# Gate tiles through ScalarE's queue, and DMA additions moved from the weight sums to the branch merge

## The chip, the cores and the metric

One core of a Trainium2 chip runs the whole kernel. The metric is the time of one execution on the device, in microseconds (us). The engines that matter here are TensorE (PE; PEld is its weight load), VectorE (DVE), ScalarE (ACT), GpSimd (POOL) and SyncE (SP). SP, ACT and POOL each have a queue from which they issue DMA transfers; a transfer issued from POOL's queue can add to its destination instead of overwriting it.

## What is computed

One layer of a hybrid decoder for 512 prompt tokens and 8 sample tokens (520 columns). The part that the change touches is the merge of the two token mixers:

```python
mix = jax.nn.sigmoid(g_a) * (o_a @ w_proj_gmlp) + jax.nn.sigmoid(g_b) * (o_b @ w_proj_nsa)
x = x + mix @ w_out
```

`o_a` and `o_b` have 1024 channels, `mix` has 2048. Everything is fp32. A product is made of three TensorE passes over operands that are split into a high part and a rest: high by high, high by rest, rest by high. ScalarE writes the high part of a weight tile (`hi`), VectorE subtracts it from the tile to get the rest (`lo`).

## The kernel before

Activations stay in SBUF as 16 tiles of 128 channels by 520 columns. Weights stream from HBM into the four slots of `w_raw` (512 KB each) by SP's queue.

**Pairs.** A stretch of the kernel works in 22 *pairs* (class `Pair`, number `n`). Each pair multiplies a 2 by 2 block of weights by a 2 by 2 block of operands with seven products instead of eight (the Winograd form of Strassen's scheme), so it needs four sums of weight quarters: `a11+a21`, `a22` plus that, `a21+a22`, and `a12` plus the second. They are the helper `st_sums` with step 0 to 3, on VectorE. Pairs 0 to 13 make gate columns `g_a` and `g_b`, whose sigmoids are stored to the DRAM tensor `merge_d`. Pairs 14 to 21 are the eight *parts* 0 to 7 (`p.part = n - 14`). Parts 0 to 3 are the four quarters `q` of the gMLP projection; their results lie in `mix_a[q]`. Parts 4 to 7 are the four quarters of the sparse-attention projection; their results lie in `b_f`. `N_PROJ = 8`, `N_ST = 14`, `N_PAIRS = 22`.

**The seven products of a pair** run in a fixed order on TensorE. Product `k` waits for `ff_lo` to reach `p.e + k + 1`, that is for the rest of weight entry `k`. The helper `ring_in(p, k)` exists twice: on ScalarE it writes the high part of entry `k`, on VectorE the rest. Entries 0, 1 and 6 are raw slots; 2 and 5 come from the buffer `st_sum` (the second and the fourth sum); 3 and 4 are sums in place in `w_raw`. An entry's buffer is one of three, so it is free when the product three entries earlier is done. ScalarE's `st_copy(p, 0..3)` and VectorE's `st_added(p, 0..2)` drain PSUM; product 4 waits for `st_copy(p, 1)`, product 3 for `st_added(p, 0)`.

**Two sums by DMA.** From pair `N_SUMMED = 12` on (`loaded_sums`), the third and the fourth sum are not made on VectorE: `low_sum` and `wide_sum` on POOL's queue load the same weight quarter once more from HBM and add it to `w_raw[:, 2]` and to `st_sum`. `wide_sum` may start when the rest of entry 2 is written, and entry 5 waits for its landing (semaphore `wide_summed`).

**Gates.** `load_gates(p)` on POOL's queue brings the four gate tiles of a part from `merge_d` to SBUF (1040 KB), into `g_in0`, `g_in1` or `g_late`, once the gates that lay there before are used. POOL's loop issues them in the same in-order queue, right behind `low_sum` of the next pair and ahead of `wide_sum` of the next pair. For part 4 two of them stand there one behind the other.

**Merge.** VectorE's `gate(p, t_)` multiplies two result tiles by their gates. From part 4 on, `merge(p, t_)` on VectorE then adds the two tiles of `mix_a` to those of `b_f`; ScalarE's `b_hi_in` and VectorE's `b_lo_in` split the sum into the operand of the output projection. In parts 5 to 7 these belong to the part before (`old`), and they stand in the instruction order between the weight entries: on VectorE gate 0 ahead of entry 2, merge 0 ahead of entry 3, gate 1 and merge 1 ahead of entry 5, `b_lo_in` ahead of and behind entry 6; on ScalarE `b_hi_in(old, 0)` between entry 4 and `st_copy(p, 1)`, `b_hi_in(old, 1)` between entry 6 and `st_copy(p, 3)`. Part 7 itself is gated, merged and split behind the last pair. After that the output projection (L1010) starts; its fourth chunk of weights waits for the last `b_lo_in`.

Of the kernel before, what the change touches and what calls it, by code (L numbers as in the profile page):

```python
# [57 lines left out]
N_ST = 14  # L58
# [6 lines left out]
U_PROJ = U_GATE + 2 * M_ST  # L65
N_PROJ = 8
N_PAIRS = N_ST + N_PROJ
N_SUMMED = 12
U_OUT = U_PROJ
U_FF = U_OUT + MB  # L70
UNITS = U_FF
# [62 lines left out]

def base_of(g, k):

    first = 2 * (N_PAIRS + N_SUMMED) if COUNTS[k] == "sums" else N_PAIRS * U_COUNTS[k]
    return first if whole(g, 0) else BODY_TOTAL[k] * g + (first + FIRST_TOTAL[k] - BODY_TOTAL[k])


# [4 lines left out]
class Pair:  # L145


    def __init__(self, n):
        self.n, self.part = n, n - N_ST
        self.phase, self.q = divmod(self.part, N_PROJ // 2)  # L150
        self.e, self.used, self.copied, self.c21, self.read, self.sums = (n * c for c in U_COUNTS)
        self.loaded_sums, turn = n >= N_SUMMED, n - N_SUMMED
        if self.loaded_sums:
            self.sums = 4 * N_SUMMED + 2 * turn
            self.summed = 16 * turn + 16

    def ring(self, k):

# [147 lines left out]
def build(nc, t):  # L306
    with ExitStack() as ctx:
# [455 lines left out]
        def gates_home(p):  # L763
            return g_late if p.part == N_PROJ // 2 else g_in[p.part % 2]
# [823 lines left out]
        def _(act):  # L1588
# [239 lines left out]

            def b_hi_in(p, t_):

                act.wait_ge(b_mixed, 2 * p.q + t_ + 1)
                run(mixed_part(b_hi, p, t_), mixed_part(b_f, p, t_), ACT.Copy).then_inc(b_split, 1)

            def st_scaled(j):
# [100 lines left out]
            ring_in(p, 0, (chunk_done, CH * (U_PROJ - 1) + 2))  # L1935
            ring_in(p, 1, (chunk_done, CH * U_PROJ))

            def first_free(p, k):

                return (b_ready, 2) if p.ring(k) == LATE and p.last_free(k) is None else None  # L1940

            def st_pair(p):
                old = Pair(p.n - 1) if p.n else None
                js = slice(2 * p.part - 2, 2 * p.part)
                if old:
                    st_c21(old)
                ring_in(p, 2, None if old else (chunk_done, CH * U_PROJ))
                if p.part == 0:
                    gm_hi(T3)
                st_copy(p, 0)  # L1950
                ring_in(p, 3, None if old else (chunk_done, CH * U_PROJ))
                if p.part == -1:
                    gm_hi(B11)
                if p.part == 0:
                    gm_hi(B22)
                if p.part in (1, 2):
                    nsa_hi(B11, js)
                ring_in(p, 4)
                if p.part > 4:
                    b_hi_in(old, 0)  # L1960
                if not old:
                    gate_out(2 * M_ST - 1)
                if p.part == -1:
                    gm_hi(B21)
                if p.part == 0:
                    gm_hi(T4)
                if p.part in (1, 2):
                    nsa_hi(B21, js)
                if p.part == 3:
                    nsa_hi(T2)  # L1970
                if old and p.part < 0:
                    st_tanh(old, 0)
                st_copy(p, 1)
                ring_in(p, 5)
                if old and p.part < 0:
                    st_tanh(old, 1)
                if p.part in (1, 2):
                    nsa_hi(B22, js)
                if p.part == 3:
                    nsa_hi(T3)  # L1980
                st_copy(p, 2)
                ring_in(p, 6)
                if p.part > 4:
                    b_hi_in(old, 1)
                if p.part == -1:
                    gm_hi(T2)
                if p.part == 0:
                    st_tanh(old, 0)
                if p.part in (1, 2):
                    nsa_hi(T1, js)  # L1990
                if p.part == 3:
                    nsa_hi(T4)
                st_copy(p, 3)
                if p.part < N_PROJ - 1:
                    to = Pair(p.n + 1)
                    ring_in(to, 0, first_free(to, 0))
                    if p.part == -1:
                        gm_hi(T1)
                    if p.part == 0:
                        st_tanh(old, 1)  # L2000
                    ring_in(to, 1, first_free(to, 1))
# [200 lines left out]
        def _(dve):  # L2202
# [640 lines left out]
            def merge(p, t_):  # L2843

                dve.wait_ge(gated, KP + 2 * p.part + t_ + 1)
                y = st_out(p, t_)
                dve.tensor_tensor(y, y, mix_a[p.q][:, t_:4:2, :], ALU.add).then_inc(b_mixed, 1)

            def st_pair(p):
# [3 lines left out]
                if old:  # L2853
# [24 lines left out]
                    if p.part == 4:  # L2878
                        gate(older, 1)
                    if p.part > 4:  # L2880
                        merge(old, 0)
                    ring_in(p, 3)
                if not p.loaded_sums:
                    st_sums(p, 3)
# [22 lines left out]
                    gate(older, 1)  # L2907
                if p.part == 4:
                    gate(old, 0)
                if p.part > 4:  # L2910
                    gate(old, 1)
                    merge(old, 1)
                if old and p.part < -1:
                    st_scale(old, 1)
                elif not old:
# [372 lines left out]
        def _(pool):  # L3288
# [205 lines left out]
            def wide_sum(p):  # L3494

                pool.wait_ge(ff_lo, p.e + 3)
                pool.dma_start(st_sum[:, :], t["w_st"][4 * p.n + 1], accum_op=ALU.add).then_inc(wide_summed, 16)

            def load_gates(p):
                for t_ in range(2):  # L3500
                    pool.wait_ge(g_stored[t_], 64 * (p.q + 1))
                pool.dma_start(gates_home(p)[:, :, :], merge_d.rearrange("(q k t) p n -> t q p k n", k=4, t=2)[
                    p.phase][p.q]).then_inc(g_loaded[p.part % 2], 16)

            for n in range(N_SUMMED - 2):
                for p in range(2):
# [2 lines left out]
            for n in range(N_SUMMED - 1, N_PAIRS):  # L3509
                p, old, to = Pair(n), Pair(n - 1), Pair(n + 1)  # L3510
                if p.loaded_sums:
                    wide_sum(p)
                if p.part <= 0:
                    gate_half(M_ST + n - 1, 0, st_out(old, 0))
                if p.part < 0:
                    gate_half(M_ST + n - 1, 1, st_out(old, 1))
                if p.part < N_PROJ - 1:
                    low_sum(to)
                if p.part == 0:
                    gate_half(M_ST + n - 1, 1, st_out(old, 1))  # L3520
                    pool.wait_ge(ff_used, old.used + NP)
                    load_gates(p)
                if p.part == 1:
                    pool.wait_ge(mix_lo, GM_DONE)
                    load_gates(p)
                if p.part in (2, 3):
                    pool.wait_ge(gated, KP + 2 * p.part - 2)
                    load_gates(p)
                if p.part == 3:
                    pool.wait_ge(ff_used, p.used + NP)  # L3530
                    load_gates(to)
                if p.part in (4, 5, 6):
                    pool.wait_ge(gated, KP + (8, 6, 12)[p.part - 4])
                    load_gates(to)
            pool.wait_ge(b_ready, N_PROJ)
            steps.did(pool.memset(acc_x[:, :], 0.0))

# [187 lines left out]
```

## Time and profile before

| | us |
|---|---|
| median of 3 runs | 2603.17 |
| lowest and highest | 2601.89, 2608.93 |
| the profiled execution's own time | 2605.25 |
| its span, from the first to the last instruction | 2603.8 |
| mean granted TensorE clock, share of full speed | 0.996 |

A profile is one execution. Times in its rows count from the start of the span. A line such as `1038.38 0.80 PE L1403 ... [6.27 <-DVE w_lo L2752]` says: at 1038.38 us an instruction of line 1403 began on PE and ran 0.80 us; before it PE stood idle for 6.27 us, which ended when the VectorE instruction of line 2752 that wrote `w_lo` signalled. Buffer numbers are left out in the names, and buffers that lie in the same memory can appear under the name of another (`a_hi`, `late_hi` and `w_hi` are all weight buffers in this stretch).

### The profile page before, as it was taken

How to read it: one execution, taken by the hardware profiler on the slowest of the kernel's cores; microseconds unless marked ns; L12 is line 12 of the kernel's file. 1: busy time of each engine (PE TensorE's matmuls, PEld its weight loads, DVE VectorE, ACT ScalarE, POOL GpSimd, SP SyncE). 2: the span in 40 equal slices, each digit the busy share in tenths (PEclk: the TensorE clock that was granted, in tenths of full speed). 3: DMA queues.
4: the chain of work that ended last, by engine and by line, in shares of the span. 5: the costliest groups of instructions: out<-in, count | busy, mean ns of one | idle time of the engine just before them, and what ended most of it. 6: DMA issues, size and time to landing. Idle time of an engine off the chain costs nothing. (4 is left out here: it accounts for less than half of the span.)

```text
span 2603.8 us, 56700 instructions
## 1 busy us (share of the span) xinstructions
PE 2573.6 (99%) x21295; PEld 2544.3 (98%) x21295; DVE 2019.4 (78%) x2903; ACT 1448.5 (56%) x2441; POOL 479.1 (18%) x641
## 2 busy tenths in 40 slices
PE   9999999999999998999999999999999999999998
PEld 9999999999999998999999999999999999999998
DVE  6455646668777787865688889888898888898888
ACT  6445436556444464432366666566666665666656
POOL 2001350001121221123302121121211211212113
PEclk9999999999999999999999999999999999999999
DMA  6633552213343466643336675665756657667568
GB/s 212 203 113 115 165 172 74 66 53 129 129 143 132 146 181 194 187 139 132 131 106 151 164 175 141 169 156 153 182 144 168 163 145 173 152 164 174 140 171 178
DMA packets 128089, 389.45 MB, mean 150 GB/s; under 512 B 14450, under 2 KB 16114, under 8 KB 127696
## 3 DMA queue, kind: packets, MB, share of 16 engines
q1 hardware_dynamic: 69328, 245.36, 28.0%
q0 software_dynamic: 55456, 136.73, 24.7%
q10 hardware_dynamic: 3168, 5.45, 0.6%
q8 instruction: 95, 1.56, 0.2%
q14 instruction: 42, 0.34, 0.0%
HBM read 302.77 MB, written 91.00 MB: 151 GB/s over the span
## 5 line engine op out<-in xcount | busy, mean ns | idle before, releaser
L3017 DVE TENSOR_TENSOR w_lo<-w_raw,w_hi 128x1024 fp32r<-128x1024 f32 x351 | 428.7, 1223 | 104.6 <-ACT w_hi L2031 104.0
L2031 ACT ACTIVATE w_hi<-w_raw 128x1024 fp32r<-128x1024 f32 x352 | 370.9, 1062 | 200.9 <-PE aux L1454 69.1
L1454 PE MATMUL aux<-at_t,w_hi 128*128 128x260 f32 x2016 | 368.0, 282 | 0.2 <-DVE w_lo L3017 0.2
L2208 DVE TENSOR_TENSOR w_lo<-w_raw,w_hi 128x512 fp32r<-128x512 f32 x216 | 158.8, 738 | 257.2 <-ACT w_hi L1599 256.5
L1518 PE MATMUL aux<-fb_mid,w_hi 128*128 128x260 f32 x1920 | 352.2, 284 | 1.4 <-DVE w_lo L3017 1.1
L1599 ACT ACTIVATE w_hi<-w_raw 128x512 fp32r<-128x512 f32 x216 | 135.2, 628 | 316.1 <-PE mm L1010 293.9
L1454 PEld LDWEIGHTS aux<-at_t,w_hi 128*128 128x128 f32 x2016 | 310.6, 188 | 0.4 <-DVE w_lo L3017 0.4
L1518 PEld LDWEIGHTS aux<-fb_mid,w_hi 128*128 128x128 f32 x1920 | 295.1, 188 | 2.7 <-DVE w_lo L3017 1.3
L1454 PE MATMUL aux<-at_t,w_lo 128*128 128x260 f32 x1008 | 284.5, 282 | 0.0
L1518 PE MATMUL aux<-fb_mid,w_lo 128*128 128x260 f32 x960 | 270.7, 282 | 0.0
L1518 PE MATMUL mm<-fb_mid,w_hi 128*128 128x260 f32 x1440 | 263.9, 282 | 0.0
L1010 PE MATMUL mm<-a_hi,w_hi 128*128 128x260 f32 x1216 | 254.5, 291 | 0.0
L1010 PE MATMUL mm<-a_hi,w_lo 128*128 128x260 f32 x1216 | 244.8, 283 | 0.0
L1010 PE MATMUL mm<-a_lo,w_hi 128*128 128x260 f32 x1216 | 244.4, 283 | 0.0
L1518 PEld LDWEIGHTS mm<-fb_mid,w_hi 128*128 128x128 f32 x1440 | 222.0, 188 | 0.0
L3579 POOL TENSOR_TENSOR cell<-cell 128x1 f32<-128x1 f32 x62 | 20.8, 335 | 1054.0 <-ACT y_mid L2084 1042.1
L1454 PE MATMUL mm<-at_t,w_hi 128*128 128x260 f32 x1120 | 204.8, 283 | 0.7 <-ACT hid L2067 0.7
L1518 PE MATMUL mm<-fb_mid,w_lo 128*128 128x260 f32 x720 | 203.7, 283 | 0.0
L1010 PEld LDWEIGHTS mm<-a_hi,w_hi 128*128 128x128 f32 x1216 | 187.9, 189 | 5.6 <-issue 3.8
L1454 PEld LDWEIGHTS aux<-at_t,w_lo 128*128 128x128 f32 x1008 | 189.6, 188 | 0.0
L1010 PEld LDWEIGHTS mm<-a_lo,w_hi 128*128 128x128 f32 x1216 | 187.4, 188 | 0.0
L1010 PEld LDWEIGHTS mm<-a_hi,w_lo 128*128 128x128 f32 x1216 | 187.4, 188 | 0.0
(600 smaller groups left out, 6865.8 us busy)
## 6 DMA issues: line engine op xcount, KB each, us to landing
w_raw<-in_w_ff SPq DMA_DIRECT2D x256, 512.0 KB, 3.6
out_y_t<-y_mid POOLq DMA_DIRECT2D x120, 520.0 KB, 8.0
w_raw<-in_w SPq DMA_DIRECT2D x110, 512.0 KB, 3.7
w_raw<-in_w_st SPq DMA_DIRECT2D x88, 512.0 KB, 5.0
g_in<-merge_d POOLq DMA_DIRECT2D x7, 1040.0 KB, 10.0
w_raw<-in_w_st POOLq DMA_DIRECT2D x10, 512.0 KB, 5.4
st_sum<-in_w_st POOLq DMA_DIRECT2D x10, 512.0 KB, 8.5
merge_d<-z POOLq DMA_DIRECT2D x18, 260.0 KB, 4.0
```

The source lines that it names most:

```text
L1010: last = pe.matmul(mm[:, 2 * v + h, 0:HT], w, a[:, kt, h * HT:(h + 1) * HT], start=first and k == 0 and part == 0, stop=final and k == CK ...
L1454: last = pe.matmul(dst, w, at_of(j)[:, e:e + HT], start=FRESH[b] and j == 0 and part == 0, stop=j == KP - 1 and part == 2, skip_group_chec ...
L1518: last = pe.matmul(dst, w, fb[:, j, e:e + HT], start=FRESH[b] and j == 0 and part == 0, stop=j == 1 and part == 2, skip_group_check=not FR ...
L1599: run(w_hi[:, c, :], raw(u, c), ACT.Copy).then_inc(hi_split, 1)
L2031: run(hi_of(p, k), source(p, k), ACT.Copy).then_inc(ff_hi, 1)
L2208: dve.tensor_tensor(w_lo[:, c, :], raw(u, c), w_hi[:, c, :].bitcast(F32), ALU.subtract).then_inc(lo_split, 1)
L3017: dve.tensor_tensor(lo_of(p, k), source(p, k), hi_of(p, k).bitcast(F32), ALU.subtract).then_inc(ff_lo, 1)
L3579: pool.tensor_tensor(cell[:, 2:3], cell[:, 0:1], cell[:, 1:2], ALU.mult).then_inc(cell_step, 1)
```

## The change

Three things are changed together.

1. `load_gates` moves from POOL's queue to ScalarE's. ScalarE issues the gates of each part from inside that part, behind the high part of entry 5 (behind entry 6 in part 3).
2. In parts 5, 6 and 7 (`n >= N_MERGED = 19`) no sum is added by DMA: VectorE makes all four (`st_sums` 2 and 3 as in pairs 0 to 11).
3. In parts 5 to 7 the merge of the part before leaves VectorE: `merged` on POOL's queue adds the two tiles of `mix_a` to those of `b_f` by a DMA from SBUF to SBUF, and `b_hi_in` waits for its landing. Gate 1 moves up to the place where merge 0 stood. Part 7 is still merged on VectorE.

```diff
--- before.py
+++ after.py
@@ -65,7 +65,7 @@
 U_PROJ = U_GATE + 2 * M_ST
 N_PROJ = 8
 N_PAIRS = N_ST + N_PROJ
-N_SUMMED = 12
+N_SUMMED, N_MERGED = 12, N_ST + 5
 U_OUT = U_PROJ
 U_FF = U_OUT + MB
 UNITS = U_FF
@@ -134,7 +134,7 @@
 
 def base_of(g, k):
 
-    first = 2 * (N_PAIRS + N_SUMMED) if COUNTS[k] == "sums" else N_PAIRS * U_COUNTS[k]
+    first = Pair(N_PAIRS).sums if COUNTS[k] == "sums" else N_PAIRS * U_COUNTS[k]
     return first if whole(g, 0) else BODY_TOTAL[k] * g + (first + FIRST_TOTAL[k] - BODY_TOTAL[k])
 
 
@@ -149,10 +149,9 @@
         self.n, self.part = n, n - N_ST
         self.phase, self.q = divmod(self.part, N_PROJ // 2)
         self.e, self.used, self.copied, self.c21, self.read, self.sums = (n * c for c in U_COUNTS)
-        self.loaded_sums, turn = n >= N_SUMMED, n - N_SUMMED
-        if self.loaded_sums:
-            self.sums = 4 * N_SUMMED + 2 * turn
-            self.summed = 16 * turn + 16
+        self.loaded_sums, turn = N_SUMMED <= n < N_MERGED, n - N_SUMMED
+        self.sums = 4 * n - 2 * min(max(turn, 0), N_MERGED - N_SUMMED)
+        self.summed = 16 * turn + 16
 
     def ring(self, k):
 
@@ -1828,7 +1827,10 @@
 
             def b_hi_in(p, t_):
 
-                act.wait_ge(b_mixed, 2 * p.q + t_ + 1)
+                if p.part == N_PROJ - 1:
+                    act.wait_ge(b_mixed, t_ + 1)
+                else:
+                    act.wait_ge((low_summed, wide_summed)[t_], Pair(p.n + 1).summed)
                 run(mixed_part(b_hi, p, t_), mixed_part(b_f, p, t_), ACT.Copy).then_inc(b_split, 1)
 
             def st_scaled(j):
@@ -1935,6 +1937,23 @@
             ring_in(p, 0, (chunk_done, CH * (U_PROJ - 1) + 2))
             ring_in(p, 1, (chunk_done, CH * U_PROJ))
 
+            GATES_USED = {2: 2, 3: 4, 5: 8, 6: 6, 7: 12}
+
+            def load_gates(p):
+
+                for t_ in range(2):
+                    act.wait_ge(g_stored[t_], 64 * (p.q + 1))
+                if p.part == 0:
+                    act.wait_ge(ff_used, Pair(N_ST - 1).used + NP)
+                elif p.part == 1:
+                    act.wait_ge(mix_lo, GM_DONE)
+                elif p.part == 4:
+                    act.wait_ge(ff_used, Pair(p.n - 1).used + NP)
+                else:
+                    act.wait_ge(gated, KP + GATES_USED[p.part])
+                act.dma_start(gates_home(p)[:, :, :], merge_d.rearrange("(q k t) p n -> t q p k n", k=4, t=2)[
+                    p.phase][p.q]).then_inc(g_loaded[p.part % 2], 16)
+
             def first_free(p, k):
 
                 return (b_ready, 2) if p.ring(k) == LATE and p.last_free(k) is None else None
@@ -1972,6 +1991,8 @@
                     st_tanh(old, 0)
                 st_copy(p, 1)
                 ring_in(p, 5)
+                if p.part >= 0 and p.part != 3:
+                    load_gates(p)
                 if old and p.part < 0:
                     st_tanh(old, 1)
                 if p.part in (1, 2):
@@ -1980,6 +2001,8 @@
                     nsa_hi(T3)
                 st_copy(p, 2)
                 ring_in(p, 6)
+                if p.part == 3:
+                    load_gates(p)
                 if p.part > 4:
                     b_hi_in(old, 1)
                 if p.part == -1:
@@ -2878,7 +2901,7 @@
                     if p.part == 4:
                         gate(older, 1)
                     if p.part > 4:
-                        merge(old, 0)
+                        gate(old, 1)
                     ring_in(p, 3)
                 if not p.loaded_sums:
                     st_sums(p, 3)
@@ -2907,9 +2930,6 @@
                     gate(older, 1)
                 if p.part == 4:
                     gate(old, 0)
-                if p.part > 4:
-                    gate(old, 1)
-                    merge(old, 1)
                 if old and p.part < -1:
                     st_scale(old, 1)
                 elif not old:
@@ -3496,11 +3516,11 @@
                 pool.wait_ge(ff_lo, p.e + 3)
                 pool.dma_start(st_sum[:, :], t["w_st"][4 * p.n + 1], accum_op=ALU.add).then_inc(wide_summed, 16)
 
-            def load_gates(p):
-                for t_ in range(2):
-                    pool.wait_ge(g_stored[t_], 64 * (p.q + 1))
-                pool.dma_start(gates_home(p)[:, :, :], merge_d.rearrange("(q k t) p n -> t q p k n", k=4, t=2)[
-                    p.phase][p.q]).then_inc(g_loaded[p.part % 2], 16)
+            def merged(p, t_):
+
+                pool.wait_ge(gated, KP + 2 * p.part + t_ + 1)
+                y = st_out(p, t_)
+                pool.dma_start(y, mix_a[p.q][:, t_:4:2, :], accum_op=ALU.add).then_inc((low_summed, wide_summed)[t_], 16)
 
             for n in range(N_SUMMED - 2):
                 for p in range(2):
@@ -3510,28 +3530,17 @@
                 p, old, to = Pair(n), Pair(n - 1), Pair(n + 1)
                 if p.loaded_sums:
                     wide_sum(p)
+                if p.part > 4:
+                    for t_ in range(2):
+                        merged(old, t_)
                 if p.part <= 0:
                     gate_half(M_ST + n - 1, 0, st_out(old, 0))
                 if p.part < 0:
                     gate_half(M_ST + n - 1, 1, st_out(old, 1))
-                if p.part < N_PROJ - 1:
+                if n + 1 < N_MERGED:
                     low_sum(to)
                 if p.part == 0:
                     gate_half(M_ST + n - 1, 1, st_out(old, 1))
-                    pool.wait_ge(ff_used, old.used + NP)
-                    load_gates(p)
-                if p.part == 1:
-                    pool.wait_ge(mix_lo, GM_DONE)
-                    load_gates(p)
-                if p.part in (2, 3):
-                    pool.wait_ge(gated, KP + 2 * p.part - 2)
-                    load_gates(p)
-                if p.part == 3:
-                    pool.wait_ge(ff_used, p.used + NP)
-                    load_gates(to)
-                if p.part in (4, 5, 6):
-                    pool.wait_ge(gated, KP + (8, 6, 12)[p.part - 4])
-                    load_gates(to)
             pool.wait_ge(b_ready, N_PROJ)
             steps.did(pool.memset(acc_x[:, :], 0.0))
```

## Rows read from the trace of the kernel before

**Rows 1.** The page, busy time of each engine.

```profile
PE 2573.6 (99%) x21295; PEld 2544.3 (98%) x21295; DVE 2019.4 (78%) x2903; ACT 1448.5 (56%) x2441; POOL 479.1 (18%) x641
```

**Rows 2.** Stretches: pair 13; 15 to 17; 18; 19; 20; 21. Length, busy by engine, PEclk, DMA.

```profile
908.50:928.60 20.10, 20.10 (x170) 20.10 (x169) 18.61 (x20) 14.03 (x18) 7.11 (x8) 1.00 0.69 184
948.70:1017.20 68.50, 63.08 (x510) 62.48 (x509) 53.95 (x54) 36.71 (x48) 9.18 (x12) 0.98 0.67 193
1017.20:1046.70 29.50, 22.93 (x168) 22.45 (x166) 19.54 (x20) 9.68 (x12) 4.97 (x6) 0.88 0.63 185
1046.70:1067.00 20.30, 20.30 (x172) 20.30 (x171) 17.44 (x17) 11.73 (x14) 0.84 (x1) 1.00 0.66 201
1067.00:1094.40 27.40, 23.14 (x169) 22.85 (x169) 21.54 (x22) 11.68 (x14) 4.10 (x5) 0.88 0.57 156
1094.40:1118.20 23.80, 21.88 (x170) 21.67 (x169) 18.27 (x19) 11.99 (x16) 0.87 (x1) 0.93 0.66 187
```

**Rows 3.** Timeline of PE, pair 18 and the start of the output projection.

```profile
1038.38 0.80 PE L1403 MATMUL mm<-nsa_t,w_hi 128*128 128x260 f32 x2 [6.27 <-DVE w_lo L2752]
1038.98 0.42 PE L1403 MATMUL mm<-nsa_t,w_lo 128*128 128x260 f32 x1
...
1118.26 0.40 PE L1010 MATMUL mm<-b_hi,w_hi 128*128 128x260 f32 x2
```

**Rows 4.** Timeline of POOL: DMA issues in pairs 13 and 18.

```profile
912.29 0.88 POOL L3497 DMA_DIRECT2D st_sum<-in_w_st  x1 [4.18 <-DVE a_lo L2752]
...
1018.74 0.79 POOL L3502 DMA_DIRECT2D g_in<-merge_d  x1 [0.20 <-issue]
1019.51 0.80 POOL L3502 DMA_DIRECT2D g_late<-merge_d  x1
1022.94 0.91 POOL L3497 DMA_DIRECT2D st_sum<-in_w_st  x1 [2.62 <-DVE w_lo L2752]
```

**Rows 5.** Timeline of ACT: entry 5 of pairs 13 and 18.

```profile
917.73 1.07 ACT L1907 ACTIVATE a_hi<-st_sum 128x1024 fp32r<-128x1024 f32 x1
...
1036.01 1.06 ACT L1907 ACTIVATE w_hi<-st_sum 128x1024 fp32r<-128x1024 f32 x1 [9.56 <-DMA st_sum<-in_w_st]
```

**Rows 6.** The page's DMA issues: queue, count, size, median us to landing.

```profile
out_y_t<-y_mid POOLq DMA_DIRECT2D x120, 520.0 KB, 8.0
...
g_in<-merge_d POOLq DMA_DIRECT2D x7, 1040.0 KB, 10.0
w_raw<-in_w_st POOLq DMA_DIRECT2D x10, 512.0 KB, 5.4
st_sum<-in_w_st POOLq DMA_DIRECT2D x10, 512.0 KB, 8.5
```

**Rows 7.** Line 912, SP's 84 weight loads among the pairs: time to landing.

```profile
DMA to landing us min/median/max: 3.0/5.0/10.3
```

**Rows 8.** Timeline of DVE, pair 20 and the end of pair 21.

```profile
1068.70 1.22 DVE L2765 TENSOR_TENSOR st_sum<-w_raw 128x1024 f32<-128x1024 f32 x1
1069.83 1.24 DVE L2841 TENSOR_TENSOR b_f<-b_f,g_in 128x1040 f32<-128x1040 f32 x1
1071.05 1.22 DVE L2752 TENSOR_TENSOR w_lo<-st_sum,w_hi 128x1024 fp32r<-128x1024 f32 x1
1072.19 1.24 DVE L2847 TENSOR_TENSOR b_f<-b_f,mix_a 128x1040 f32<-128x1040 f32 x1
...
1074.76 0.69 DVE L2780 TENSOR_TENSOR b_f<-b_f,mm 128x520 f32<-128x520 f32 x1
...
1116.79 1.24 DVE L2841 TENSOR_TENSOR b_f<-b_f,g_in 128x1040 f32<-128x1040 f32 x1
...
1122.86 2.47 DVE L2663 TENSOR_TENSOR b_lo<-b_f,b_hi 128x1040 fp32r<-128x1040 f32 x2
```

**Rows 9.** Timeline of ACT, pair 20.

```profile
1074.44 1.06 ACT L1832 ACTIVATE b_hi<-b_f 128x1040 fp32r<-128x1040 f32 x1
1075.73 0.60 ACT L1921 ACTIVATE b_f<-mm 128x520 f32<-128x520 f32 x1 [0.23 <-PE mm L1403]
1083.46 1.06 ACT L1907 ACTIVATE w_hi<-st_sum 128x1024 fp32r<-128x1024 f32 x1 [7.12 <-DMA st_sum<-in_w_st]
```

**Rows 10.** Line 1656, issues on ACT's own queue: duration of one, ns.

```profile
L1656 ACTq DMA_DIRECT2D out_kv_t<-z x10: 338/338/339, 56.2 to 161.2; - x10
```

## The prediction

> **What bounds the kernel now.** First the page: TensorE is busy for 99% of the span [rows 1], so a change can win only where TensorE idles or runs slowly. Next the stretches of the pairs. Pair 13 has its sums from DMA and no gates in the way: 20.1 us, all of it busy, clock 1.00 [rows 2]. That is 2.87 us a product. Against 20.1 us a pair, pairs 15 to 17 lose 68.5 - 60.3 = 8.2, pair 18 9.4, pair 19 0.2, pair 20 7.3, pair 21 3.7: 28.8 us, nearly all that this stage can give back. Part of it is clock: in pair 18 TensorE is idle for 29.5 - 22.93 = 6.6 of the 9.4 lost, and the matmuls that follow the idle time take 0.42 us with a mean granted clock of 0.88 [rows 2, 3].
>
> Then who ends the idle time. TensorE waits for the rest of entry 5 [rows 3], VectorE for its high part, and ScalarE for the landing of `wide_sum` (9.56 us in pair 18, 7.12 in pair 20) [rows 5, 9]. Last the queue: in pair 13 `wide_sum` is issued at 912.29 and ScalarE goes on at 917.73 without a wait, at most 5.4 us later. In pair 18 two gate loads go out at 1018.74 and 1019.51; `wide_sum` follows at 1022.94 and ScalarE goes on at 1036.01, 13.1 us later [rows 4, 5]. Five of the seven pairs that lose time show this chain; the reader is to see 5.4 us without gates and a median of 8.5 with them [rows 6].
>
> **The change part by part.** T is the start of a pair's first product.
>
> *Gates leave POOL's queue (parts 0 to 4).* Nothing then stands between `low_sum` and `wide_sum`. In pair 18 `wide_sum` is issued at T + 5.7; landed in 5.4 it is there at T + 11.1. High part 1.06 and rest 1.22 make T + 13.4; product 5 is due at 5 x 2.87 = 14.4. One us to spare, where 13.1 us brought the rest to about T + 21. So the loss goes in pairs 15 to 18: 8.2 + 9.4 = 17.6 us. Bounds: 0 if `wide_sum` lands as late as now, 17.6 if it lands in 5.4 to 6.4. I take 17.6, since pair 13 is the same pair without gates. Late next would be the rest of product 6, whose entry is a raw slot and early.
>
> *The issue on ScalarE.* An issue on its queue takes 0.34 us [rows 10], eight of them 2.7 us. Each stands behind the high part of entry 5 and ahead of `st_copy(p, 2)`, which can't run before T + 11.5 and is due at T + 14.4: hidden by products 4 and 5. Without that cover it costs 0.34 a pair. Its own waits (stores of gates, earlier gates used) name work that is done by then: part 2's gate 1 stands ahead of entry 5 on VectorE, which product 5 needs anyway. Behind it wait `st_copy(p, 2)`, entry 6 and `b_hi_in`.
>
> *The gates' traffic.* The 1040 KB now start at about T + 11 to 13 and meet the loads of the next pair's slots. The latest of these, the fourth slot, is issued behind entry 6 at about T + 15.5 and is read by the next pair's second sum. That sum 1.22, high part 1.06 and rest 1.22 must be done at the next T + 5.7, so the slot may land at the next T + 2.2, which is 6.8 us after its issue. Loads in this stretch land in 3.0 to 10.3, median 5.0 [rows 7]. Bounds: 0 to 3.5 us a pair; I take 0, since the median is below 6.8.
> By the Trainium skill ("DMA: Bandwidth & Descriptors", "Issuing engines are not separate DMA queues") transfers from any engine share the same 16 DMA engines, and another issuer saves only issue time. By that the 1040 KB cost the same wherever they are issued; here they also move in time, behind `wide_sum`, which the rule does not price. It is the second rival below.
>
> *Parts 5 to 7, VectorE.* Two sums (1.13 us from start to start) come, two merges (1.14 to 1.15) go: equal work [rows 8]. A pair then has on VectorE seven rests at 1.14, four sums at 1.13, three additions at 0.69, two gates and two `b_lo_in` at 1.15: 19.2 us of 20.1.
>
> *Parts 5 to 7, the new wait.* `wide_sum` is gone here, and with it 0.2 + 7.3 + 3.7 = 11.2 us. In its place ScalarE waits at `b_hi_in(old, 0)` for a DMA that starts behind gate 0. Queued behind it on ScalarE are `st_copy(p, 1)`, which product 4 needs, entry 5, and the gates. Call L the time from gate 0's end to the merge's landing. The rest of entry 5 can start L + 1.06 + 0.60 + 1.06 = L + 2.7 after gate 0 [rows 9]. Meanwhile VectorE has rest 2, gate 1, rest 3, sum 4, an addition and rest 4: 1.14 + 1.15 + 1.14 + 1.13 + 0.69 + 1.14 = 6.4. So it idles L - 3.7, and its round takes 19.2 + L - 3.7 = 15.5 + L. Above L = 4.6 that is longer than TensorE's 20.1, and VectorE sets the pace.
> The first of the three pairs has a start ahead: VectorE can begin behind the previous sixth product (T - 2.9), and after high part and rest 1, two sums and gate 0 it is at T - 2.9 + 1.06 + 1.22 + 1.13 + 1.13 + 1.24 = T + 2.9; product 4 is due at T + 11.5, and `st_copy(p, 1)` is ready at T + 2.9 + L + 1.66. It loses nothing up to L = 6.9.
> No DMA of before goes from SBUF to SBUF with an addition. Nearest rows: additions into SBUF of 512 KB, 5.4 alone, 13.1 at worst [rows 4 to 6]; additions of 520 KB from SBUF to DRAM, median 8.0 [rows 6]. At L = 5.4 the round is 20.9, at 8.0 23.5, at 13.1 28.6. I take 5.8: destination and size are those of the 5.4, with a little for the second merge right behind. Round 21.3: 1.2 us lost in pairs 20 and 21 each, 2.4, and 0.2 for clock. Saved in the three pairs: 11.2 - 2.6 = 8.6. With L = 5.4 it is 9.6; with 8.0, 1.2 + 3.4 + 3.4 and about 1 us of clock for each stall (pairs 15 to 17: 5.4 idle, 8.2 lost, three stalls), 11: nothing saved.
>
> *End of the stage.* Part 7's gates now start inside pair 21 at about T + 12.3 and land some 8 to 10 us later (10.0 was the median behind POOL [rows 6]), T + 20.3 to 22.3. Before, gate 0 ran at 1116.79, 1.5 us ahead of the first output product at 1118.26; the last `b_lo_in` ended at 1125.33, and the fourth chunk was due at 1118.26 + 3 x 2.87 = 1126.9, 1.6 us later [rows 3, 8]. At T + 20.3 the gates are 1.7 us later than gate 0 was: 0.1 lost. At T + 22.3, 2.1. I take 0.5.
>
> **Sum.** 17.6 + 8.6 - 0.5 = 25.7 us. The profiled execution took 2605.25, so 2579.6; it lies 2.1 above the median of the runs shown, on which the sum gives 2603.2 - 25.7 = 2577.5, said as 2578.
>
> **The rivals.**
> - *The merge by DMA is slow (L of 8 and more).* For it: 8.0 is the median of the same bytes out of SBUF, and two merges follow each other. Against it: 5.4 into SBUF. The last three pairs then lose about what they lose now: 2603.2 - 17.6 + 0.5 = 2586.
> - *The gates only move their delay.* For it: loads that share with gates take up to 10.3 us [rows 7]. Against it: pair 18 moves 185 GB/s at a DMA share of 0.63 [rows 2], so there is room; pair 13's 184 hold with no loss. If the fourth slot lands in 8 us, the next pair loses 1.2, in seven pairs some 8: 2586. The skill's rule speaks for this rival.
> - *Slower: the same slot lands at 10.3 in every pair.* Then 3.5 and about 1 us of clock for seven pairs make 31: 2609. It decides from 6.8 us on and ends above before from some 9.5 us on. Against it: 10.3 is the maximum of 84, a median of 5.0.
> - *The change does not do what it says: `wide_sum` is late because of SP's loads, not because of gates.* Then pairs 15 to 18 stay as they are and only the last three win: 2603.2 - 8.1 = 2595. Against it: pairs 13 and 14 have the same SP loads and no wait.
>
> **How the numbers follow.** Chances: forecast 0.64, slow merge 0.14, moved delay 0.13, no effect of the gates 0.05, slower 0.04. The forecast's own range is 2574 (all 28.8 gone) to 2584. The range 2572 to 2595 takes in the run spread of before below and the first, second and fourth cases above; it leaves out the slower one and tails of the others, about 0.15. What a measurement can tell from no change is 0.3%, 8 us. Faster: forecast and the first two rivals, less their tails, and half of the fourth, 0.90; same 0.06; slower 0.04.
>
> **What the profile would show.** Right: stretches of pairs 15 to 18 of 20.1 to 20.6 us at clock 1.00; ScalarE without a wait for `st_sum`; `wide_sum` landing in 5 to 6.5 us; gates on ACT's queue, landing by the next T + 1; three merges of two each on POOL with landings near 5.8; a ScalarE wait of a few us for them ahead of `b_hi`, VectorE idle by 2 us ahead of entry 5, pairs 20 and 21 at about 21.3. Wrong: VectorE's second sum waiting for a `w_raw` load (moved delay); `b_hi` waiting 4 us and more (slow merge); the first output products idling for `b_lo` (late gates of part 7).

## The result, and the profile after

The changed kernel takes 2586.12 us (median, 2585.00 to 2587.42), the kernel before 2603.01 beside it: a ratio of 0.9931 [0.9914, 0.9948]. It is faster by 16.9 us, where 25.7 were forecast (2578). The stated range of 2572 to 2595 holds the measured time; the forecast's own range of 2574 to 2584 does not. The profiled execution took 2585.23 us (2579.6 forecast for it) with a span of 2583.8, 20.0 less than that of before; 8.2 of them are TensorE's busy time, the rest idle time gone; compare [rows 1]:

```profile
PE 2565.4 (99%) x21295; PEld 2535.6 (98%) x21295; DVE 2019.6 (78%) x2903; ACT 1451.5 (56%) x2441; POOL 470.0 (18%) x633
```

The same stretches as in [rows 2], cut at the first product of each pair: pairs 15 to 17, 18, 19, 20, 21.

```profile
948.88:1009.45 60.57, 60.57 (x507) 60.44 (x505) 55.83 (x56) 37.41 (x47) 7.88 (x10) 1.00 0.77 214
1009.45:1029.60 20.15, 20.15 (x171) 20.15 (x169) 17.21 (x17) 10.26 (x12) 0.87 (x1) 1.00 0.76 211
1029.60:1050.79 21.19, 20.52 (x170) 20.14 (x168) 16.64 (x16) 12.25 (x15) 2.41 (x2) 1.00 0.69 200
1050.79:1074.69 23.90, 21.15 (x169) 20.44 (x169) 19.28 (x18) 11.38 (x14) 2.36 (x2) 1.00 0.62 178
1074.69:1098.03 23.34, 20.95 (x171) 20.44 (x169) 19.96 (x20) 11.89 (x16) 2.36 (x2) 1.00 0.63 183
```

Pairs 15 to 18 run without a gap, as forecast: 0.2 us lost there instead of 17.6. The last three lose 1.1 + 3.8 + 3.2 = 8.1 us, where 2.6 were forecast and 11.1 were lost before. So in the two profiled executions the gates of parts 0 to 4 brought 17.3 of their 17.6 us and the last three pairs 3.0 instead of 8.6.

The page's DMA issues of the changed kernel answer to [rows 6]: `wide_sum` lands in 5.5 us instead of 8.5.

```profile
g_in<-merge_d ACTq DMA_DIRECT2D x7, 1040.0 KB, 7.4
...
st_sum<-in_w_st POOLq DMA_DIRECT2D x7, 512.0 KB, 5.5
b_f<-mix_a POOLq DMA_DIRECT2D x6, 520.0 KB, 7.0
```

Where TensorE stands still in pair 20 (timeline of PE): at the third product, for the rest of entry 2, and at the fourth, for `st_added(p, 0)`. Neither was forecast as a place of loss.

```profile
1058.42 0.51 PE L1402 MATMUL mm<-nsa_t,w_hi 128*128 128x260 f32 x2 [1.43 <-DVE w_lo L2775]
...
1062.54 0.48 PE L1402 MATMUL mm<-nsa_t,w_hi 128*128 128x260 f32 x2 [1.00 <-DVE b_f L2803]
```

VectorE's idle time in the same pair (timeline of DVE): 1.60 us behind the chain of the first merge, as forecast (1.6 for a merge that lands 5.3 us behind gate 0's end), but also 2.47 for the second merge's `b_hi` and 0.43 for the next pair's slot 0. ScalarE's rows show what it waited for.

```profile
1065.13 1.22 DVE L2775 TENSOR_TENSOR w_lo<-st_sum,w_hi 128x1024 fp32r<-128x1024 f32 x1 [1.60 <-ACT w_hi L1909]
...
1071.12 1.24 DVE L2686 TENSOR_TENSOR b_lo<-b_f,b_hi 128x1040 fp32r<-128x1040 f32 x1 [2.47 <-ACT b_hi L1834]
...
1073.40 1.23 DVE L2775 TENSOR_TENSOR late_lo<-w_raw,late_hi 128x1024 fp32r<-128x1024 f32 x1 [0.43 <-ACT late_hi L1909]
```
```profile
1048.42 1.06 ACT L1909 ACTIVATE w_hi<-w_raw 128x1024 fp32r<-128x1024 f32 x1 [1.99 <-DMA w_raw<-in_w_st]
...
1062.59 1.08 ACT L1834 ACTIVATE b_hi<-b_f 128x1040 fp32r<-128x1040 f32 x1 [4.17 <-DMA b_f<-mix_a]
...
1070.01 1.08 ACT L1834 ACTIVATE b_hi<-b_f 128x1040 fp32r<-128x1040 f32 x1 [2.77 <-DMA b_f<-mix_a]
...
1072.31 1.06 ACT L1909 ACTIVATE late_hi<-w_raw 128x1024 fp32r<-128x1024 f32 x1 [0.73 <-DMA w_raw<-in_w_st]
```

These waits look like the whole cause. The experiments show that the merges' two are not all of it.

### The profile page after: what moved, and what is told of

Read it like the earlier page. It is cut to its first block and busy times, and to the rows that moved or that the text cites. A ratio compares the mean times of both kernels' runs of the same rounds, so it can differ in the third digit from the quotient of the medians.

```text
span 2583.8 us, 56703 instructions
## 1 busy us (share of the span) xinstructions
PE 2565.4 (99%) x21295; PEld 2535.6 (98%) x21295; DVE 2019.6 (78%) x2903; ACT 1451.5 (56%) x2441; POOL 470.0 (18%) x633
```

## The experiments

"Lost" is what the pairs take above 20.12 us each, from the starts of their first products, in the one profiled execution of each run; that of e6 is 3.4 us above the run's median and that of e5 1.8. The kernel before loses 17.6 and 11.1.

| run | median us | ratio to before | lost, pairs 15 to 18 | pairs 19 to 21 |
|---|---|---|---|---|
| changed kernel | 2586.12 | 0.9931 [0.9914, 0.9948] | 0.2 | 8.1 |
| e1 gates only | 2577.44 | 0.9891 [0.9876, 0.9906] | 0.6 | 0.0 |
| e2 merge swap only | 2607.13 | 1.0001 [0.9992, 1.001] | 19.9 | 12.8 |
| e3 gates on POOL, behind `wide_sum` | 2584.48 | 0.9917 [0.9903, 0.993] | 4.6 | 2.8 |
| e4 gates on ScalarE, early | 2599.55 | 0.9978 [0.9967, 0.9988] | 15.0 | 7.8 |
| e5 changed, late parts' gates early | 2582.55 | 0.9914 [0.9901, 0.9928] | 0.1 | 5.9 |
| e6 changed, merges on VectorE | 2583.53 | 0.9918 [0.9904, 0.9931] | 0.9 | 7.8 |
| e7 sums and merges by DMA | 2587.97 | 0.9935 [0.9922, 0.9949] | 0.8 | 9.8 |
| e8 changed kernel again | 2584.67 | 0.9922 [0.9908, 0.9935] | 0.3 | 8.0 |
| e9 no merge | 2584.46 | 0.9915 [0.9898, 0.9931] | 0.4 | 7.0 |
| e10 first merge only | 2583.09 | 0.9911 [0.9895, 0.9928] | 0.3 | 5.7 |
| e11 second merge only | 2586.39 | 0.9922 [0.9906, 0.9939] | 0.5 | 8.5 |
| e12 no merge, no late gates | 2579.39 | 0.9903 [0.9886, 0.9919] | 0.3 | 1.6 |

### The two halves apart: e1 and e2

e1 is the kernel before with the gates on ScalarE's queue, sums and merges untouched:

```diff
 # ScalarE, in each part (entry 6 in part 3)
                 ring_in(p, 5)
+                if p.part >= 0 and p.part != 3:
+                    load_gates(p)
 # POOL: every wait and load_gates removed
```

> The kernel before with the gate loads moved to ScalarE's queue, and nothing else: two sums by DMA in all parts, merges on VectorE. In the changed kernel the parts' eight pairs take 169.3 us, 8.3 above eight clean ones; 8.1 of these lie in the last three pairs. Theory A (the merge by DMA is what still costs: with wide_sum landing in 5.4 us the last three pairs would be as clean as 15 to 18): eight pairs 161 to 163 us, time some 6 to 8 us below the changed kernel, about 2579. Theory B (the last three pairs needed the swap, because the gates' bytes or VectorE's 19.2 us a pair hold them up anyway): last three pairs lose 8 us or more, time 2586 or above.

e2 is the changed kernel with the gates put back on POOL's queue, at their old places.

> The changed kernel with the gate loads back on POOL's queue where they stood (behind low_sum of the next pair, in the last parts behind the two merges): only the swap of sums and merges is left. Both theories: pairs 15 to 18 lose their 17 to 18 us again. If the swap by itself wins what the prediction gave it (8.6 us in the last three pairs), the time is about 2594; if it wins only the 3.3 us that the last three pairs gained in the changed kernel, about 2600; if the gates behind the merges delay the next part, 2603 or more.

e1 takes 2577.44 us, 0.9891 [0.9876, 0.9906], near the 2579 of its theory A (the cause that this names is taken up below), and apart from 0.5 us in pair 15 all seven pairs run at TensorE's pace. Windows of pairs 15 to 17, 18, 19, 20, 21 of e1:

```profile
948.97:1009.86 60.89, 60.84 (x506) 60.51 (x505) 56.14 (x57) 37.32 (x47) 7.87 (x10) 1.00 0.78 213
1009.86:1030.01 20.15, 20.15 (x171) 20.15 (x170) 17.21 (x17) 10.23 (x12) 1.73 (x2) 1.00 0.74 211
1030.01:1050.12 20.11, 20.11 (x170) 20.11 (x169) 19.45 (x19) 12.04 (x14) 1.72 (x2) 1.00 0.73 210
1050.12:1070.24 20.12, 20.12 (x171) 20.12 (x169) 19.43 (x19) 12.16 (x14) 1.73 (x2) 1.00 0.75 210
1070.24:1090.39 20.15, 20.15 (x170) 20.15 (x169) 19.41 (x20) 12.34 (x16) 0.86 (x1) 1.00 0.87 235
```

e2 takes as long as before, 1.0001 [0.9992, 1.001], the time of the last of its three cases. Its chain of [rows 4, 5] is unchanged in pair 18 (timelines of POOL and of ACT): two gates, `wide_sum` behind them landing 12.2 us after its issue, ScalarE waiting 8.68 us.

```profile
1021.33 0.79 POOL L3501 DMA_DIRECT2D g_in<-merge_d  x1 [0.20 <-issue]
1022.10 0.78 POOL L3501 DMA_DIRECT2D g_late<-merge_d  x1
1025.52 0.91 POOL L3496 DMA_DIRECT2D st_sum<-in_w_st  x1 [2.64 <-DVE w_lo L2754]
```
```profile
1037.76 1.06 ACT L1909 ACTIVATE w_hi<-st_sum 128x1024 fp32r<-128x1024 f32 x1 [8.68 <-DMA st_sum<-in_w_st]
```

So the whole gain, and more, is the gates'. The other part of the change gives back 7 to 9 us of it (2586.1, and 2584.7 in e8, against 2577.4), 8.1 of them in the last three pairs.

### Queue or moment: e3 and e4

The gates changed their queue and their moment at once. e3 leaves them on POOL's queue but puts each part's gates behind that part's own `wide_sum`. e4 sends them by ScalarE, but at the head of the next pair, ahead of `wide_sum` in time (part 4's stay at e1's place). Both keep sums and merges of before.

```diff
 # e3, POOL                          # e4, ScalarE, ahead of entry 2
     wide_sum(p)                     +    if 0 < p.part < 5:
+if p.part >= 0:                     +        load_gates(old)
+    load_gates(p)                   +    if p.part > 4:
                                     +        load_gates(p)
```

> The kernel before with each part's gates still on POOL's queue but behind that part's own wide_sum instead of ahead of the next one; sums and merges as before. Queue-order theory (what counts is that nothing stands ahead of wide_sum in its queue; ScalarE's queue is not needed): within 2 us of the kernel that moves the gates to ScalarE, pairs 15 to 18 clean. If the other queue matters by itself: the next low_sum lands late behind the gates, pairs 15 to 18 lose 1 us each or more.

> The gates on ScalarE's queue but at the time at which POOL issued them, at the head of the next pair and so ahead of wide_sum in time (part 4 excepted, which stays behind entry 5); sums and merges as before. Queue-order theory: wide_sum lands in 5.4 to 6 us all the same, pairs 15 to 18 clean, time as with the gates moved. Shared-engines theory (the same 16 DMA engines carry the bytes, whichever queue issues them): wide_sum lands in 7 to 9.5 us as before, pairs 15 and 17 lose 3 to 4 us each and pairs 20 and 21 again 4 to 7, time 2590 to 2600.

e3 has most of the gain without ScalarE: 0.9917 [0.9903, 0.993]. e4, on ScalarE's queue, has little: 0.9978 [0.9967, 0.9988]. Line `wide_sum`, duration of its issues and time to landing, in e3 and in e4:

```profile
L3497 POOL DMA_DIRECT2D st_sum<-in_w_st x10: 841/854/892, 891.7 to 1081.8; - x10
DMA to landing us min/median/max: 5.3/5.3/6.0
```
```profile
L3520 POOL DMA_DIRECT2D st_sum<-in_w_st x10: 862/866/891, 892.2 to 1093.6; - x10
DMA to landing us min/median/max: 5.3/7.5/8.9
```

In e4 nothing stands ahead of `wide_sum` in POOL's queue, and it is late all the same: 1040 KB issued 3.9 to 5.6 us ahead of it, on another queue, delay it to 7.1 to 8.9 in pairs 15 to 21. The rule of the Trainium skill ("DMA: Bandwidth & Descriptors", "Issuing engines are not separate DMA queues"), that transfers of all issuers share the same DMA engines, agrees: changing the issuer alone did not free `wide_sum`. To be in flight together is not enough, though: in e3 the gates are issued 0.5 to 0.6 us behind `wide_sum` in five of the seven pairs 15 to 21, and it lands in 5.3 to 6.0.

And the queue is not without effect. What holds TensorE most in e4 is not `wide_sum` but `low_sum`, in pair 15 for 4.20 us, in pair 17 for 3.59: in pair 15 ScalarE waits 5.12 us for its landing, and on VectorE `st_added(p, 0)`, which the fourth product needs, stands behind the rest of that entry (timelines of PE and of ACT).

```profile
961.80 0.56 PE L1403 MATMUL aux<-a_hi 128*128 128x260 f32 x1 [4.20 <-DVE mix_a L2803]
```
```profile
958.67 1.06 ACT L1907 ACTIVATE a_hi<-w_raw 128x1024 fp32r<-128x1024 f32 x1 [5.12 <-DMA w_raw<-in_w_st]
```

Line `low_sum`, the seven of pairs 15 to 21, in the kernel before and in e4:

```profile
L3492 POOL DMA_DIRECT2D w_raw<-in_w_st x7: 839/850/865, 948.5 to 1092.6; - x7
DMA to landing us min/median/max: 5.2/5.3/5.5
```
```profile
L3515 POOL DMA_DIRECT2D w_raw<-in_w_st x7: 857/859/865, 948.8 to 1088.4; - x7
DMA to landing us min/median/max: 5.3/7.8/9.8
```

In the kernel before, the gates follow `low_sum` on the same queue, 0.55 to 0.62 us behind it in five of the pairs, and do not delay it. In e4 they follow on ScalarE's queue: issued 0.24 to 0.51 us behind (five pairs) they leave it landing in 6.9 to 9.8 us, issued 1.4 us behind (two pairs) in 5.3. So e4's 15.0 and 7.8 are not the price of the late `wide_sum` alone.

e3 stays 7 us short of e1, where its theory allowed 2, and loses 4.6 in pairs 15 to 18. In five of the seven pairs its gates go out 2 to 4 us earlier than in e1, and the slot loads beside them land in a median of 5.7 us instead of 4.8; that the one makes the other is argued, the late slots are shown. ScalarE's waits for DMA in pairs 15 to 21 (who waited, for what: total, times, longest) in e1 and in e3: the slots cost it 5.0 us in e1 and 19.4 in e3.

```profile
ACT w_hi L1907 <- DMA w_raw<-in_w_st: 2.5, 4, 1.0
ACT a_hi L1907 <- DMA w_raw<-in_w_st: 2.1, 3, 0.8
...
ACT late_hi L1907 <- DMA w_raw<-in_w_st: 0.4, 1, 0.4
```
```profile
ACT w_hi L1907 <- DMA w_raw<-in_w_st: 10.9, 7, 3.1
...
ACT a_hi L1907 <- DMA w_raw<-in_w_st: 4.8, 3, 2.2
ACT late_hi L1907 <- DMA w_raw<-in_w_st: 3.7, 2, 2.5
```

### What the last three pairs lose: e5, e6, e7, e8

e5 is the changed kernel with the gates of parts 5 to 7 at the head of their pair, away from the second merge. e6 puts the merges back on VectorE but leaves all four sums there, so that no DMA adds in these parts. e7 is e1 with both merges by DMA besides the sums by DMA, so that VectorE has the least work. e8 is the changed kernel again.

```diff
 # e5, ScalarE                        # e6, ScalarE                     # e7, POOL
+if p.part > 4:                       -act.wait_ge(..., summed)         +merged(old, 0)
+    load_gates(p)                    +act.wait_ge(b_mixed, ...)         wide_sum(p)
 ring_in(p, 2)                        # VectorE: merge(old, 0/1) back   +merged(old, 1)
```

> The changed kernel with the gates of parts 5 to 7 issued at the head of their pair, where no transfer is in flight, instead of behind entry 5. In the changed kernel the last three pairs lose 8.1 us; the first merge of each lands in 5.0 to 5.1 us, the second, which meets the gates and three weight loads, in 8.9 to 10.2. Theory A (a traffic jam: gates and weight loads delay the second merge and the next pair's first slot, and VectorE waits for both): second merge in 6 to 7 us, last three pairs lose 2 us or less, time about 2580. Theory B (it is the chain of gate, first merge, high part, copy, entry 5 that holds VectorE up, at whatever landing): VectorE still idles 1.6 us ahead of entry 5, the last three pairs lose 5 us or more, time 2583 or above.

> The changed kernel with the merges of parts 4 to 6 back on VectorE as well, so that in parts 5 to 7 VectorE makes four sums and two merges a pair (19.2 + 2.3 = 21.5 us of work against 20.1 of TensorE) and nothing there waits for a DMA addition. If only VectorE's work counts: 1.4 us lost a pair, some 3 to 4 us in the last three (the first has a start ahead), time about 2581, better than the changed kernel. If the wait for the DMA merge costs less than 2.3 us of VectorE work, as the change supposes: last three pairs lose more than 8.1, time 2586 or above.

> Gates on ScalarE's queue, two sums by DMA in all parts, and the merges of parts 4 to 6 by DMA too: VectorE is relieved to 16.9 us a pair, the DMA engines get 1.06 MB more. If VectorE's load is what makes the wait for the merge show: last three pairs nearly clean, time 2578 to 2580. If the wait itself is what costs (product 4 behind copy, copy behind the merge): loss of 1 to 2 us a pair stays, 2581 to 2584. If the bytes are too many: wide_sum lands in 8 us or more, loss of 8 us or more, 2586 and above.

> The changed kernel once more, as the yardstick for the three others on the same chip: 0.993 of before, about 2586.

Against e8 (0.9922 [0.9908, 0.9935], 8.0 us lost) e5 loses 5.9, e6 7.8 and e7 9.8; their times lie too close to e8's to be told apart, and the pairs' lengths carry the reading. e5 comes out nearer to its theory B: VectorE still idles 1.6 us ahead of entry 5, and the second merge lands in 8.4 to 9.0 us without the gates beside it, where theory A had 6 to 7. e6 has 21.5 us of VectorE work a pair by the prediction's own prices (19.2, and two merges) and no merge to wait for, and in its profiled execution comes out as the changed kernel does; neither of its two cases (3 to 4 lost, more than 8.1 lost) is met. In e7 the least work on VectorE loses the most, much as its third case had it: more bytes are in flight (pair 20: slot loads land in up to 10.5 us, `wide_sum` in 7.9). That the bytes make the loss is argued; the first merge also stands ahead of `wide_sum` in POOL's queue there, which goes out about 2 us later than in e1. The price of the merges' DMA seemed to be what is left, and the next three runs were made to show it.

### Without the merges: e9, e10, e11

These leave out both merges of parts 4 to 6, the second, and the first; `b_hi` then goes on when the gate is done. All else is the changed kernel.

```diff
-act.wait_ge((low_summed, wide_summed)[t_], Pair(p.n + 1).summed)
+act.wait_ge(gated, KP + 2 * p.part + t_ + 1)
 # POOL
-merged(old, t_)
```

> Leaves out both merges of parts 4 to 6: the tiles of mix_a are not added, b_hi goes on when the gate is done; gates, loads and VectorE's four sums stay as in the changed kernel. Theory (the 8.1 us that the last three pairs still lose come from waits on the two merges and from what the merges do to the loads beside them): VectorE has 19.4 us of work a pair against TensorE's 20.1 and waits for nothing else, so the three pairs lose 0.5 us at most and the time is about 2577, a ratio near 0.989. Rival (four sums on VectorE, or gates and loads by themselves, cost the time): at least 3 us stay lost, 2580 or more.

> Leaves out the second merge of parts 4 to 6 (one tile of mix_a is not added), keeps the first as a DMA. Theory: the chain behind the first merge idles VectorE 1.6 us a pair, as forecast, so its round is 19.4 + 1.6 = 21.0 and pairs 20 and 21 lose 0.9 each; with 520 KB less beside them gates and slot loads land earlier and add little: some 2 us lost, 2578.5. That would be the 2.6 us that the prediction gave the three pairs. Rival (the first merge's chain is the main cost, the second merge is incidental): 6 us or more lost, 2582.5 and up.

> Leaves out the first merge of parts 4 to 6, keeps the second as a DMA. Theory: ScalarE has no wait ahead of entry 5, so VectorE's 1.6 us of idle time there goes; the second merge, without the 520 KB of the first, lands some 2 us earlier than the 10.2 of the changed kernel, but VectorE gets to it 1.6 us earlier too, so about 2 us of wait stay: pairs 20 and 21 lose 1.4 each, some 3 us in all, 2579.5. The two merges by themselves then cost less than both together (8.1), the rest being that they share the transfers' time. Rival (the second merge alone makes all of the loss): 6 us or more, 2582.5 and up.

The theory falls in all three: 2584.46, 2583.09 and 2586.39, where 2577, 2578.5 and 2579.5 were expected. Without any merge the three pairs still lose 7.0 of the 8.1 us. VectorE's idle time did not go; it moved to slot 0. ScalarE's timeline in e9, the high parts of slot 0 of pairs 20 and 21, and the SP issue between them with its time to landing:

```profile
1048.19 1.06 ACT L1909 ACTIVATE w_hi<-w_raw 128x1024 fp32r<-128x1024 f32 x1 [2.33 <-DMA w_raw<-in_w_st]
...
1071.44 1.06 ACT L1909 ACTIVATE late_hi<-w_raw 128x1024 fp32r<-128x1024 f32 x1 [2.49 <-DMA w_raw<-in_w_st]
```
```profile
L911 SPq DMA_DIRECT2D w_raw<-in_w_st x1: 328/328/328, 1063.3 to 1063.3; - x1
DMA to landing us min/median/max: 8.1/8.1/8.1
```

e10 shows the other side: in its pair 20 the gates, held up by the first merge's `b_hi`, are issued at 1063.28, behind slot 0's load (1062.52) and not ahead of it. The load lands in 4.5 us, and pair 21 loses 1.8 us instead of 3.1. In pair 19 of the same run the gates go out 0.55 us ahead of that load; it lands in 7.8, and pair 20 loses 3.3.

What e9 shows is a closed round. Slot 0 lands; ScalarE's high part and then VectorE's rest 0, all four sums, both gates, two additions and rests 1 to 4 follow, 15.1 us without a gap; then SP may load slot 0 again, and the load takes 8.1: 23.2 us, and pair 21 takes 23.26. In the changed kernel it is 1048.42 to 1063.56, and 8.7 for the load: 23.9, the length of its pair 20.

```profile
L911 SPq DMA_DIRECT2D w_raw<-in_w_st x1: 327/327/327, 1063.6 to 1063.6; - x1
DMA to landing us min/median/max: 8.7/8.7/8.7
```

From slot 0's high part in pair 20 to that in pair 21, the timeline of ACT gives 23.19 us in e6 (1050.24 to 1073.43) and 24.16 in e11 (1048.88 to 1073.04); the pairs last 23.36 and 24.15.

e5 has the same round without gates beside the load: slot 0's high part at 1049.22, the next load at 1064.36, its landing 7.6 us later, beside the merges and two other slot loads; 22.7 us, and pair 20 takes 22.87.

```profile
L911 SPq DMA_DIRECT2D w_raw<-in_w_st x1: 328/328/328, 1064.4 to 1064.4; - x1
DMA to landing us min/median/max: 7.6/7.6/7.6
```

Why the load now falls together with the gates, the merges and two other slot loads stands in SP's loop, which is the same in both kernels:

```python
a12_read = (1, (ff_lo, p.e + 2)) if p.loaded_sums else (1, (ff_sum, p.sums + 4))
a21_read, rest = (2, (ff_lo, p.e + 4)), ((0, (ff_lo, p.e + 5)), (3, (ff_lo, p.e + 7)))
order = (a12_read, a21_read) if p.loaded_sums else (a21_read, a12_read)
```

With sums by DMA, slot 1 is free at rest 1, slot 2 at rest 3, slot 0 at rest 4. With sums on VectorE, slot 1 is held until the fourth sum, and rests 3 and 4 stand behind one and two sums more. In pair 20, issues of slots 1, 2 and 0 in e1 (line SP, time to landing of all four loads of the pair) come at T + 0.4, + 6.5 and + 8.3, T being 1050.12; in the changed kernel slots 2, 1 and 0 come at T + 9.9, + 11.0 and + 12.8, within 2.9 us and together with the gates and the second merge.

```profile
L912 SPq DMA_DIRECT2D w_raw<-in_w_st x4: 328/328/328, 1050.5 to 1064.6; - x4
DMA to landing us min/median/max: 3.8/5.1/5.4
```
```profile
L911 SPq DMA_DIRECT2D w_raw<-in_w_st x3: 327/327/328, 1060.7 to 1063.6; - x3
DMA to landing us min/median/max: 6.1/8.4/8.7
```

### The round tested: e12

e12 is e9 with the gates of parts 5 to 7 not loaded (VectorE's gate products take the tiles of parts 3 and 4 that still lie in SBUF); every engine's order and work stay.

```diff
-if p.part >= 0 and p.part != 3:
+if 0 <= p.part < 5 and p.part != 3:
     load_gates(p)
```

> The run without the two merges, and in parts 5 to 7 the gates are not loaded either (the gate multiplication there takes the tiles of parts 3 and 4 that still lie in SBUF); every engine's order and work stay. New theory, after the run without merges still lost 7.0 us in the last three pairs: the round goes through weight slot 0. From its landing (1048.16 there) VectorE has rest 0, four sums but one, two gates, two additions and rests 1 to 4 to do before SP may load it again (1063.33), 15.17 us, and the load takes 8.09 beside the gates and two other slot loads that the sums on VectorE release at the same moment: 23.26, the length of pair 21. Without the gates' 1040 KB the slot should land in 4.5 to 5.5 us, the round is 19.7 to 20.7, and the three pairs lose 0 to 1.5 us: 2577.5 to 2579. Rival (VectorE's order and its four sums set the round, whatever the loads do): the stalls of 1.6 and 1.2 us at the third and the fourth product stay, 2584.5.

It takes 2579.39 us, 0.9903 [0.9886, 0.9919], just above the 2577.5 to 2579 of the theory and 5 below the rival. Slot 0's loads of pairs 19 and 20 land in 5.0 and 4.1 us, ScalarE waits for no load in these pairs, and the pairs last 20.6 to 20.7 (windows of pairs 19, 20, 21):

```profile
1029.59:1050.28 20.69, 20.37 (x170) 20.19 (x169) 19.21 (x19) 11.81 (x14) 0.00 (x0) 1.00 0.32 102
1050.28:1070.91 20.63, 20.35 (x170) 20.17 (x169) 19.16 (x19) 11.94 (x14) 0.00 (x0) 1.00 0.31 102
1070.91:1091.57 20.66, 20.39 (x170) 20.21 (x169) 19.11 (x20) 12.11 (x16) 0.00 (x0) 1.00 0.38 127
```

The 0.5 us a pair that stay are one stall of 0.3 at the fourth product, for `st_added(p, 0)`, and longer matmuls (TensorE is busy 20.35 to 20.39 instead of 20.12): VectorE's order, without any late load, still costs 1.6 us in the three pairs. With the same order and no merges, 5.4 us go with the gates' bytes.

## Why the prediction was right, and which step failed

- **Gates leave POOL's queue, 17.6 us: right, for a reason that needs a word.** Pairs 15 to 18 lose 0.2, and e1 shows the gain by itself. Leaving the queue is neither needed nor enough: with the gates behind `wide_sum` on the same queue (e3) it lands in 5.3 to 6.0, with the gates ahead of it on another (e4) in 7.1 to 8.9.
- **The issue on ScalarE, nothing: right.** An issue takes 0.37 us (0.34 forecast), and e1 has no gap from it.
- **The gates' traffic, 0 a pair: right with sums by DMA, wrong without.** In e1 slot loads land in 3.4 to 7.2 us, and no pair but the first of them is longer than 20.2. In the last three pairs, with the merges left out, the same bytes are worth 5.4 us (e12 against e9). The rival "the gates only move their delay" was half right there: the late slot is slot 0, not the fourth slot whose 6.8 us of room were worked out, and it stays late when the gates are moved away and the merges stay (7.6 in e5). The room that the prediction read from a mean DMA share of 0.63 says little: e9's pair 20 has 0.41, and its slot 0 lands in 8.1.
- **Parts 5 to 7, VectorE: the step that failed.** "Two sums come, two merges go: equal work" holds for the total, but the sums stand ahead of rests 3 and 4 and read the slots themselves. Counted from the pair's start, slot 1 is loaded 10.7 us later, slot 2 3.4 and slot 0 4.4. Where SP's loads were spread over the pair they now come in one bunch. So the term of 2.6 lost (1.2 in each of pairs 20 and 21, 0.2 for clock) had no part for late slot loads, whose times were read from a kernel that spreads them; it measured 8.1.
- **The new wait, L = 5.8 and about 2 us idle: nearly right in size, but not alone what decides.** The first merge of each pair lands 5.0 to 5.1 us after its issue, 5.3 behind gate 0's end in pair 20, and VectorE idles 1.60, which is the prediction's formula at 5.3. The second, for whose own landing the prediction had no term, lands in 8.9 to 10.2. Yet without both (e9) 7.0 us stay lost: the round by the merges and the round by slot 0 are nearly equally long, and taking one away shows the other. Merges and late gates, taken away one by one, tell as much: with merges and no gates beside the slot loads (e5) slot 0 lands in 7.6 us and 5.9 are lost, with gates and no merges (e9) 8.1 and 7.0, with neither (e12) 4.1 and 1.6, with both (the changed kernel) 8.7 and 8.1. Either is enough to make the three bunched slot loads late, and the two do not add up. How much of e5's 5.9 is slot 0 and how much the wait for the first merge stays open.
- **End of the stage, 0.5: measured about 0.2,** one gap at the start of the output projection, in part by luck: the gates of part 7 landed at T + 22.2, the late end of the forecast, for which it had 2.1 us; pair 21 was itself 3.2 us longer.

The rival "the merge by DMA is slow" gave 2586, which is what was measured, but for another reason: its first landing was 5, not 8. The number agreeing does not make the mechanism right. The same goes for the forecast: the measured time lies in its stated range only because that range takes in the rivals.

## What to carry to other kernels

When work that reads a buffer moves from a DMA to an engine, ask when the buffer is now released, not only whether the engine's total is the same: here two sums more on VectorE in place of two merges cost nothing as work, and up to 8 us once their bunched loads met other traffic (1.6 where they met none). Where two rounds are nearly equal, a wait in the trace names the one that is longer by a little, and only leaving it out tells what it is worth. Moving a transfer helps by what it then stands behind: here gates issued ahead of a sum delayed it from either queue, gates issued about half a microsecond behind it only from another queue. The best version here is the smallest edit: e1, gates to ScalarE's queue behind entry 5 and nothing else, 2577.4 us.

## What the runs showed of the hardware

- An adding DMA of 520 KB from SBUF to SBUF lands 5.0 to 5.1 us after its issue when nothing else is in flight at its issue (the changed kernel's first merges), like the adding 512 KB from HBM with no gates ahead of them (5.2 to 5.8 in e1); with the first merge's tail, the gates and three slot loads beside it, 8.9 to 10.2, and without the gates (e5) 8.4 to 9.0.
- Its issue holds POOL for 1.17 to 1.22 us, the issue of 1040 KB of gates holds ScalarE's queue for 0.37 to 0.42.
- A 512 KB load among the pairs took between 3.1 and 8.7 us in the changed kernel, and slot 0's went from 8.1 to 4.1 us when 1040 KB issued 1.7 us ahead of it were left out (e9, e12).
- An adding 512 KB load on POOL's queue, followed by 1040 KB: 5.2 to 5.5 us when they come 0.55 to 0.62 us behind on the same queue (before), 6.9 to 9.8 when they come 0.24 to 0.51 us behind on ScalarE's, 5.3 when 1.4 us behind (e4).
